# Moving the subtraction of the low parts, the first head's rotation, the partial sums of squares and the cut of the last output tiles

## The chip, the cores and the metric

The kernel runs on one core of a Trainium2 chip. TensorE (PE) multiplies matrices, VectorE (DVE), ScalarE (ACT) and GpSimd (POOL) work on elements, and SyncE (SP), POOL and ACT issue transfers (DMA). The metric is the device time of one execution in microseconds (us).

## The reference

The program is one inference step of a trunk of two layers (width 1024). It has 592 tokens: 16 meta tokens and 512 prompt tokens in one sequence, and 8 running sequences of 8 new tokens each. Each layer computes, in float32:

```
xn = rmsnorm(x, ln_g)
q, k, v, z_a, x_b, z_b, g_a, g_b = split(xn @ w_in)
q, k = rope(q), rope(k) * DK ** -0.5
ret  = chunked retention with decay, 4 heads, state S        # q k^T * decay @ v + q @ S
o_a  = group_norm(ret) * silu(z_a)
o_b  = rglru(causal_conv(x_b)) * silu(z_b)
x   += (sig(g_a) * (o_a @ w_a) + sig(g_b) * (o_b @ w_b)) @ w_o
```

At the end comes `y = rmsnorm(x, final_gain)`. The retention states, the convolution's last rows and the recurrent vectors are outputs too.

## The kernel before, in words

Every float32 factor is split into a high part (ACT rounds it by a copy) and a low part (the value less the high part). A product is then three matmuls into the same bank: high by high, weight's low by high, weight's high by low. The tokens lie along the free axis, so a tile of 128 output features is made of two halves of 296 tokens (288 in layer 1 where the meta tokens aren't needed), each of 8 steps of three matmuls, 24 in all.

The weights come in units of 128 x 1024. SP loads unit u when unit u-4 has been used; ACT makes `w_hi`, DVE `w_lo`, three units ahead of use. Four banks of PSUM serve as a ring: a half of a tile can start only when DVE has read what stood in its bank.

A layer begins with four heads (phase R). Head 0 is special. Its q and k tiles (units 0 to 3) are made from x times gain, not yet divided by the root of the mean square, so that PE can start before that root is there. The division is put into the cosines and sines (`trig`). Meanwhile the normalised xn is made for everything that follows: DVE multiplies (`norm(k)`, one of 8 tiles, into `xnf` with two buffers), ACT copies to `xn_hi`, and POOL subtracts to get `xn_lo` (lines 597 to 602); `norm(k)` waits for the subtraction of tile k-2. The root needs the sum over all 1024 features of the squares: ACT squares 8 tiles, DVE adds them into one or two partial sums (`GROUP`), and PE multiplies these by a matrix of ones (`square_sums`), placed at the step `sums_at` of `project_first`.

In head 0 DVE turns q by the angles right after q's second tile (lines 1168, 1169), fills `qz` and `qt` (lines 1179, 1185), and does the same for k after the fourth tile. PE transposes k through PSUM (`keys`), DVE scales it (`ktok`), ACT and DVE split it (`ktok_hi`, `ktok_lo`, lines 791, 792, 1229, 1230). Then DVE signals `ktok_ready`.

What follows for the 8 running sequences goes over SP's queue, in this order for each head: three transfers `k_scr<-ktok`, a weight unit, two transfers to `kst`, three of `v_scr<-vtok`, and, when those have landed, two of `vst<-v_scr`. Only when `vst` has landed may PE start `grow(0)` (line 1729), which stands between the tiles 8 and 9 of the head. PE's queue is in order, so everything behind waits with it.

The last phase (O) projects the merged branches by w_o. In layer 1 its last four tiles (features 512 to 1023) are run first for the first half of the tokens (`n` = 0), then for the second (`n` = 1), so that the first half's root and results are made while PE works on the second. DVE's queue in that stretch holds new x, the partial sum, the reciprocal and the results of the first half, in a fixed order. After the last matmul come, one behind another: new x, its square, the sum by ones, the square root, the reciprocal, four results and their transfers.

Of the kernel before, what the change touches and what calls it, by code (L numbers as in the profile page):

```python
# [36 lines left out]
T = TP + TS  # L37
# [29 lines left out]
WARM = 10  # L67
# [8 lines left out]

def cut_of_norm(n):
    return HALVES if n < DEPTH else cut(DEPTH - 1)
# [142 lines left out]
def trunk(nc, x_in, w_units, gate_w, packs, final_gain, consts, decay, state_ret,  # L221
# [7 lines left out]
    with ctx:  # L229
# [195 lines left out]
        GROUP = [4] + [KT] * DEPTH  # L425
        NORM_AT = {1: (0, 1), 2: (2, 3), 3: (4, 5), 4: (6,), 5: (7,)}

        def buffer(n, k):
            return k % 2
# [39 lines left out]
        def _(sp):  # L469
# [77 lines left out]
            for n, (a, b) in enumerate(cut(DEPTH - 1)):  # L547
                for k in range(0, KT, 2):
                    sp.wait_ge(y_ready, n * (KT // 2) + k // 2 + 1)
                    sp.dma_start(y_out.rearrange("p (k t) -> p k t", k=KT)[:, k:k + 2, a:b], yT[:, k:k + 2, a:b])\  # L550
                        .then_inc(y_stored, 16)
# [4 lines left out]
        def _(pool):  # L556
# [13 lines left out]
            for l in range(0, DEPTH):  # L570
# [7 lines left out]
                for h in range(0, HEADS):  # L578
# [17 lines left out]
                    if h == 0:  # L596
                        for k in range(KT):
                            pool.wait_ge(xnh_ready, l * KT + k + 1)
                            apart(pool)
                            pool.tensor_tensor(xn_lo[:, k, :], xnf[:, k % 2, :], xn_hi[:, k, :].bitcast(f32), SUB)\  # L600
                                .then_inc(xn_ready, 1)
                        pool.drain()
# [90 lines left out]
        def _(act):  # L693
# [57 lines left out]
            for l in range(0, DEPTH):  # L751
# [7 lines left out]
                for h in range(0, HEADS):  # L759
# [10 lines left out]
                    for i in range(11):  # L770
# [13 lines left out]
                        if i == 2:  # L784
                            act.wait_ge(qk_ready, hh * 2 + 1)
                            act.activation(qt_hi[:, :, :], qt[:, :, :], ACT.Copy)
                            act.activation(qk_hi[:, 0:2, :], qk[:, 0:2, :], ACT.Copy)
                            act.drain().then_inc(qkh_ready, 1)
# [213 lines left out]
            for n, (a, b) in enumerate(cut(DEPTH - 1)):  # L1002
# [11 lines left out]
        def _(dve):  # L1014
# [47 lines left out]
            for k in range(KT):  # L1062
                dve.drain()
                add_square(0, k)
            first_lo(2)

            for l in range(0, DEPTH):
# [24 lines left out]

                def norm(k):

                    if k >= 2:
                        dve.wait_ge(xn_ready, l * KT + k - 1)
# [4 lines left out]
                for h in range(0, HEADS):  # L1101
# [42 lines left out]
                    for i in range(11):  # L1144
                        turn = rot_k if h == 0 and i == 3 else rot
                        if i < 4:
# [19 lines left out]
                            if i % 2:  # L1166
                                a = first if i == 1 else 0
# [5 lines left out]
                            if i == 1:  # L1173
# [14 lines left out]
                            if i % 2:  # L1188
# [28 lines left out]
                        if h == 0:  # L1217
                            for k in {2: (2, 3), 3: (4, 5), 4: (6,), 5: (7,)}.get(i, ()):
                                norm(k)
                        if i == 4:  # L1220
# [337 lines left out]
                def new_x(it, i, n):  # L1558
                    a, b = cut(l)[n]
# [25 lines left out]
            def result(n, k):  # L1585
                a, b = cut(DEPTH - 1)[n]
# [9 lines left out]
            def last_square(n, k):  # L1596
                a, b = cut(DEPTH - 1)[n]
# [22 lines left out]
        def _(pe):  # L1620
# [15 lines left out]
            def project(ph, l, it, tile, i, which=(0, 1), left=None):  # L1636
# [4 lines left out]
                for n in which:  # L1641
                    a, b = (HALVES if every else cut(l))[n]
# [58 lines left out]
            for l in range(0, DEPTH):  # L1701
                for h in range(0, HEADS):
# [68 lines left out]
                    if h == 0:  # L1771
                        project_first("R", l, h, xg_ready, 0, raw, *((10, 5, True) if l == 0 else (5, 3)))
# [174 lines left out]
            for n in range(2):  # L1947
                for i in range(4):
                    if (n, i) == (1, 1):
                        square_sums(DEPTH, (0,))  # L1950
                    project("O", DEPTH - 1, 1, ("proj", i), i, (n,))
# [106 lines left out]
```

## Time and profile before

| what | value |
|---|---|
| median of 3 runs | 1938.37 us (1937.81 to 1938.79) |
| the profiled execution | 1938.32 us, its span 1936.5 us |
| PE busy | 1918.5 us, 99% of the span |
| DVE busy | 1181.5 us, 61% |
| ACT busy | 742.3 us, 38% |
| POOL busy | 265.2 us, 14% |
| chain that ended last | PE 86%, DVE 5%, ACT 4% |

The span is the time from the first to the last instruction in the trace. The profiled execution takes 1.8 us more than its span. Busy time of PE comprises the time in which a matmul's result drains, so two matmuls overlap in the rows; the distance between two starts is the price of one in a row of many. A number in brackets at the end of a row is the engine's idle time before that instruction and what ended it. A transfer's issue is shown at the queue that issues it (SPq), its landing in the chain.

### The profile page before, as it was taken

How to read it: one execution, taken by the hardware profiler on the slowest of the kernel's cores; microseconds unless marked ns; L12 is line 12 of the kernel's file. 1: busy time of each engine (PE TensorE's matmuls, PEld its weight loads, DVE VectorE, ACT ScalarE, POOL GpSimd, SP SyncE). 2: the span in 40 equal slices, each digit the busy share in tenths (PEclk: the TensorE clock that was granted, in tenths of full speed). 3: DMA queues.
4: the chain of work that ended last, by engine and by line, in shares of the span. 5: the costliest groups of instructions: out<-in, count | busy, mean ns of one | idle time of the engine just before them, and what ended most of it. 6: DMA issues, size and time to landing. Idle time of an engine off the chain costs nothing.

```text
span 1936.5 us, 32128 instructions
## 1 busy us (share of the span) xinstructions
PE 1918.5 (99%) x13184; PEld 1797.3 (93%) x13184; DVE 1181.5 (61%) x2008; ACT 742.3 (38%) x1149; POOL 265.2 (14%) x375
## 2 busy tenths in 40 slices
PE   8999999999999999999999999999999999999998
PEld 8889898898899999999998988988988999999997
DVE  8665665565666887424486655656556678853345
ACT  5332322323336766422343223233223367754223
POOL 2221120120231200000021201202102422000000
PEclk9999999999999999999999999999999999999999
DMA  6434533453343333322255335534534533342222
GB/s 216 134 115 163 178 125 125 162 169 112 130 155 99 105 105 107 123 77 77 88 170 168 126 126 169 168 112 134 178 116 137 167 98 104 101 135 79 84 81 81
DMA packets 105856, 247.01 MB, mean 128 GB/s; under 512 B 10830, under 2 KB 51134, under 8 KB 105326
## 3 DMA queue, kind: packets, MB, share of 16 engines
q1 hardware_dynamic: 78590, 149.74, 25.0%
q0 software_dynamic: 26976, 95.22, 14.9%
q8 instruction: 104, 1.70, 0.4%
q14 instruction: 42, 0.34, 0.1%
q10 hardware_dynamic: 144, 0.00, 0.0%
HBM read 186.10 MB, written 49.12 MB: 121 GB/s over the span
## 4 chain that ended last, share of the span: by engine, by line
PE 86%; DVE 5%; ACT 4%; DVEq 1%; DMA 1%; ACTq 1%; issue 1%; SPq 0%
PE bank L1624 21%; PE bank L1626 20%; PE bank L1625 20%; PE bank L1694 5%; PE bank L1696 5%; PE bank L1695 5%; PE last L1712 1%; PE last L1694 1%; PE last L1695 1%; PE last L1696 1%; PE bank L1852 1%; PE sums L1729 1%; DVE ct L1416 1%; DVE w_lo L462 1%; DVE rr L1469 1%
## 5 line engine op out<-in xcount | busy, mean ns | idle before, releaser
L1624 PE MATMUL bank<-xn_hi,w_hi 128*128 128x296 f32 (+1 forms) x2432 | 727.5, 299 | 0.2
L1626 PE MATMUL bank<-xn_lo,w_hi 128*128 128x296 f32 (+1 forms) x2432 | 722.4, 297 | 0.0
L1625 PE MATMUL bank<-xn_hi,w_lo 128*128 128x296 f32 (+1 forms) x2432 | 721.5, 297 | 0.0
L1624 PEld LDWEIGHTS bank<-xn_hi,w_hi 128*128 128x128 f32 x2432 | 457.3, 188 | 5.9 <-issue 4.3
L1625 PEld LDWEIGHTS bank<-xn_hi,w_lo 128*128 128x128 f32 x2432 | 457.8, 188 | 0.4
L1626 PEld LDWEIGHTS bank<-xn_lo,w_hi 128*128 128x128 f32 x2432 | 456.8, 188 | 0.0
L462 DVE TENSOR_TENSOR w_lo<-w_raw,w_hi 128x1024 fp32r<-128x1024 f32 x245 | 300.3, 1228 | 184.8 <-ACT w_hi L454 177.1
L454 ACT ACTIVATE w_hi<-w_raw 128x1024 fp32r<-128x1024 f32 x245 | 257.7, 1055 | 362.2 <-DMA w_raw<-in_w_units 357.7
L1624 PE MATMUL bank<-oa_hi,w_hi 128*128 128x296 f32 (+1 forms) x512 | 153.7, 300 | 0.0
L1625 PE MATMUL bank<-oa_hi,w_lo 128*128 128x296 f32 (+1 forms) x512 | 151.9, 297 | 0.0
L1626 PE MATMUL bank<-oa_lo,w_hi 128*128 128x296 f32 (+1 forms) x512 | 151.7, 296 | 0.0
L1624 PE MATMUL bank<-ob_hi,w_hi 128*128 128x296 f32 (+1 forms) x384 | 113.9, 297 | 0.0
L1625 PE MATMUL bank<-ob_hi,w_lo 128*128 128x296 f32 (+1 forms) x384 | 113.9, 297 | 0.0
L1626 PE MATMUL bank<-ob_lo,w_hi 128*128 128x296 f32 (+1 forms) x384 | 113.8, 296 | 0.0
L1694 PE MATMUL bank<-w_hi,xn_hi 128*128 128x512 f32 x256 | 100.9, 394 | 0.7 <-DVE rot_k L1160 0.7
L1696 PE MATMUL bank<-w_lo,xn_hi 128*128 128x512 f32 x256 | 100.8, 394 | 0.0
L1695 PE MATMUL bank<-w_hi,xn_lo 128*128 128x512 f32 x256 | 100.8, 394 | 0.0
L1624 PEld LDWEIGHTS bank<-oa_hi,w_hi 128*128 128x128 f32 x512 | 96.3, 188 | 3.9 <-issue 3.9
L1625 PEld LDWEIGHTS bank<-oa_hi,w_lo 128*128 128x128 f32 x512 | 96.3, 188 | 0.0
L1626 PEld LDWEIGHTS bank<-oa_lo,w_hi 128*128 128x128 f32 x512 | 96.3, 188 | 0.0
L592 POOL DMA_DIRECT2D out_ret_s<-S x64 | 45.9, 719 | 328.9 <-DVEq L1119 183.8
L767 ACT ACTIVATE zz<-bank 128x296 f32<-128x296 f32 (+1 forms) x64 | 26.5, 414 | 119.8 <-PE bank L1626 119.2
(286 smaller groups left out, 3083.7 us busy)
## 6 DMA issues: line engine op xcount, KB each, us to landing
w_raw<-in_w_units SPq DMA_DIRECT2D x215, 512.0 KB, 3.6
S<-in_state_ret POOLq DMA_DIRECT2D x64, 512.0 KB, 4.8
out_ret_s<-S POOLq DMA_DIRECT2D x64, 512.0 KB, 6.2
w_raw<-in_w_units SPq DMA_DIRECT2D x66, 256.0 KB, 3.2
vst<-v_scr SPq DMA_DIRECT2D x8, 512.0 KB, 4.1
out_ret_p<-Sp POOLq DMA_DIRECT2D x8, 512.0 KB, 5.9
v_scr<-vtok_hi SPq DMA_DIRECT2D x16, 160.0 KB
dec<-in_decay POOLq DMA_DIRECT2D x9, 264.0 KB, 5.1
```

What stands on the lines that cost most here:

```text
L454: act.activation(w_hi[:, n % RING, :], w_raw[:, n % RING, :], ACT.Copy).then_inc(unit_hi, 1)
L462: dve.tensor_tensor(w_lo[:, n % RING, :], w_raw[:, n % RING, :], w_hi[:, n % RING, :].bitcast(f32), SUB).then_inc(unit_lo, 1)
L592: pool.dma_start(dst, S[:, s, :, :]).then_inc(s_out[s], 16)
L767: act.activation(zz[:, i - 8, a:b], psum_of("R", name)[:, 0:b - a], ACT.Tanh, scale=0.5)\
L1416: dve.scalar_tensor_tensor(ct[:, 0:wide], xpad[:, t, j:j + wide], w(j), ct[:, 0:wide], MUL, ADD)
L1469: dve.tensor_tensor_scan(rr[:, t, :], aa[:, t, :], ii[:, t, :], 0.0, MUL, ADD)
L1624: pe.matmul(ps, w_hi[:, slot, cols], x_hi, start=first, stop=False)
L1625: pe.matmul(ps, w_lo[:, slot, cols], x_hi, start=False, stop=False)
L1626: return pe.matmul(ps, w_hi[:, slot, cols], x_lo, start=False, stop=last)
L1694: pe.matmul(ps, left_hi, right_hi, start=first, stop=False)
L1695: pe.matmul(ps, left_lo, right_hi, start=False, stop=False)
L1696: return pe.matmul(ps, left_hi, right_lo, start=False, stop=last)
```

## The change

Six edits, all in the same program:

1. `xn_lo` is subtracted by DVE (`norm_lo`) instead of POOL. `norm(k)` from k = 2 on begins with a drain of DVE in place of the wait for POOL.
2. In head 0 of each layer the rotation of q, with `qz` and `qt`, moves from unit 1 to unit 2 in DVE's order, between `norm(2)` and `norm(3)`; ACT's copies `qt_hi` and `qk_hi` move behind `xn_hi` of the tiles 4 and 5.
3. In front of layer 0 the squares are added into four partial sums of two tiles instead of two of four. Four additions remain of six, and drains between them go; PE's multiplications by ones become eight from four (a float32 matmul shows as two in the trace).
4. The sum by ones stands at step 9 instead of 10 in layer 0, and at step 6 instead of 5 in layer 1.
5. PE's warming matmuls before the first real one are 12 instead of 10.
6. The last four output tiles are cut into 336 and 240 tokens instead of 288 and 288.

```diff
-WARM = 10
+WARM = 12
+LAST = ((N_META, N_META + 336), (N_META + 336, T))
 def cut_of_norm(n):
-    return HALVES if n < DEPTH else cut(DEPTH - 1)
+    return HALVES if n < DEPTH else LAST
...
-        GROUP = [4] + [KT] * DEPTH
+        GROUP = [2] + [KT] * DEPTH
...
         def buffer(n, k):
-            return k % 2
+            return k // 2 % 2 if GROUP[n] == 2 else k % 2
...
-                    if h == 0:
-                        for k in range(KT):
-                            pool.wait_ge(xnh_ready, l * KT + k + 1)
-                            apart(pool)
-                            pool.tensor_tensor(xn_lo[:, k, :], xnf[:, k % 2, :], xn_hi[:, k, :].bitcast(f32), SUB)\
-                                .then_inc(xn_ready, 1)
-                        pool.drain()
...
-                        if i == 2:
+                        if i == (2 if h else 3):
                             act.wait_ge(qk_ready, hh * 2 + 1)
                             act.activation(qt_hi[:, :, :], qt[:, :, :], ACT.Copy)
...
             for k in range(KT):
-                dve.drain()
                 add_square(0, k)
...
+                def norm_lo(k):
+
+                    dve.wait_ge(xnh_ready, l * KT + k + 1)
+                    dve.tensor_tensor(xn_lo[:, k, :], xnf[:, k % 2, :], xn_hi[:, k, :].bitcast(f32), SUB)\
+                       .then_inc(xn_ready, 1)
+
                 def norm(k):
 
                     if k >= 2:
-                        dve.wait_ge(xn_ready, l * KT + k - 1)
+                        dve.drain()
...
                         if h == 0:
-                            for k in {2: (2, 3), 3: (4, 5), 4: (6,), 5: (7,)}.get(i, ()):
+                            if i == 1:
+                                norm_lo(0)
+                                norm_lo(1)
+                            if i == 2:
+                                norm(2)
+                                rotated(0, rot, first)
+                                norm(3)
+                                queries_apart()
+                                dve.drain().then_inc(qk_ready, 1)
+                                norm_lo(2)
+                                norm_lo(3)
+                            for k in {3: (4, 5), 4: (6,), 5: (7,)}.get(i, ()):
                                 norm(k)
+                            for k in {3: (4, 5), 4: (6,), 5: (7,)}.get(i, ()):
+                                norm_lo(k)
...
-                        project_first("R", l, h, xg_ready, 0, raw, *((10, 5, True) if l == 0 else (5, 3)))
+                        project_first("R", l, h, xg_ready, 0, raw, *((9, 5, True) if l == 0 else (6, 3)))
...
-                    project("O", DEPTH - 1, 1, ("proj", i), i, (n,))
+                    project("O", DEPTH - 1, 1, ("proj", i), i, (n,), None, LAST)
```

`rotated` and `queries_apart` hold the instructions of lines 1168 to 1171 and 1174 to 1187, unchanged. The other uses of `cut(DEPTH - 1)` in the last stretch become `LAST` as well.

DVE in head 0 of layer 0, before, from the first two tiles of `xnf` to the first product with q's fellow k. `rot` is q's second tile times sine and cosine, `L462` makes `w_lo`.

```order
L1097 SCALAR_TENSOR_TENSOR xnf<-acc,lp,rstd 128x592 x2
L1168 TENSOR_TENSOR qk<-qk,rot 128x592
L1169 TENSOR_TENSOR qk<-qk,rot 128x592
L1179 TENSOR_TENSOR qz<-qk,cst 128x4x8 x4
L1185 TENSOR_TENSOR qt<-qk,cst 128x32
L462 TENSOR_TENSOR w_lo<-w_raw,w_hi 128x1024
L1155 TENSOR_TENSOR qk<-bank,trig 128x296
```

The same place after; `L465` makes `w_lo`, `L1091` is the new `xn_lo`, and `L1156` and `L1157` read the third projected tile.

```order
L1098 SCALAR_TENSOR_TENSOR xnf<-acc,lp,rstd 128x592 x2
L465 TENSOR_TENSOR w_lo<-w_raw,w_hi 128x1024
L1091 TENSOR_TENSOR xn_lo<-xnf,xn_hi 128x592 x2
L1156 TENSOR_TENSOR qk<-bank,trig 128x296
L1157 TENSOR_TENSOR qk<-bank,trig 128x296
L1156 TENSOR_TENSOR qk<-bank,trig 128x296
L1157 TENSOR_TENSOR qk<-bank,trig 128x296
L465 TENSOR_TENSOR w_lo<-w_raw,w_hi 128x1024
L1098 SCALAR_TENSOR_TENSOR xnf<-acc,lp,rstd 128x592
L1169 TENSOR_TENSOR qk<-qk,rot 128x592
L1170 TENSOR_TENSOR qk<-qk,rot 128x592
L1098 SCALAR_TENSOR_TENSOR xnf<-acc,lp,rstd 128x592
```

The weight's low part and the reading of the third tile now stand ahead of q's rotation, and each pair of `xnf` is followed by its pair of `xn_lo`.

ACT in the same head, before, from the second pair of `xn_hi` to the `w_hi` that DVE needs next (`L786` and `L787` are q's copies, `L773` is k's).

```order
L757 ACTIVATE xn_hi<-xnf 128x592 x2
L786 ACTIVATE qt_hi<-qt 128x32
L787 ACTIVATE qk_hi<-qk 128x1184
L454 ACTIVATE w_hi<-w_raw 128x1024
L757 ACTIVATE xn_hi<-xnf 128x592 x2
L773 ACTIVATE qk_hi<-qk 128x1184
L454 ACTIVATE w_hi<-w_raw 128x1024
```

And after (`L457` makes `w_hi`, `L753` `xn_hi`, `L783` is q's copy, `L769` k's):

```order
L457 ACTIVATE w_hi<-w_raw 128x1024
L753 ACTIVATE xn_hi<-xnf 128x592 x2
L782 ACTIVATE qt_hi<-qt 128x32
L783 ACTIVATE qk_hi<-qk 128x1184
L769 ACTIVATE qk_hi<-qk 128x1184
L457 ACTIVATE w_hi<-w_raw 128x1024
```

Both copies of 1184 columns now stand between the third pair of `xn_hi` and the next `w_hi`.

## Rows read from the trace of the kernel before

**Rows 1.** The page, part 1: busy time, share of the span, instructions.
```profile
PE 1918.5 (99%) x13184; PEld 1797.3 (93%) x13184; DVE 1181.5 (61%) x2008; ACT 742.3 (38%) x1149; POOL 265.2 (14%) x375
```

**Rows 2.** Waits of PE, whole span: us in total, times, longest.
```profile
PE bank L1624 <- DVE qk L1156: 1.8, 2, 1.7
PE sums L1685 <- DVE sqs L1035: 1.6, 2, 1.0
...
PE sums L1729 <- DMA vst<-v_scr: 1.0, 1, 1.0
PE sums L1743 <- DVEq L1189: 0.7, 1, 0.7
```

**Rows 3.** PE in order of time, head 0 of layer 0: start, us, what.
```profile
6.37 0.61 PE L1624 MATMUL bank<-xg_hi,w_hi 128*128 128x296 f32 x1 [0.65 <-DVE w_lo L1054]
...
80.98 0.49 PE L1729 MATMUL sums<-vst,kst 24*128 24x512 f32 x2 [0.95 <-DMA vst<-v_scr]
```

**Rows 4.** SP's queue in order of time, the same head.
```profile
65.81 0.77 SPq L502 DMA_DIRECT2D k_scr<-ktok_hi  x1
```

**Rows 5.** The chain that ended last, layer 0 and layer 1.
```profile
76.60 4.33 DMA vst<-v_scr
...
1037.24 4.14 DMA vst<-v_scr
...
1041.42 0.49 PE sums L1729
```

**Rows 6.** DVE in order of time, layer 0.
```profile
18.34 2.51 DVE L1035 TENSOR_TENSOR sqs<-sqs,sq 128x592 f32<-128x592 f32 x3 [0.77 <-ACT sq L710]
...
22.75 2.00 DVE L1019 RECIPROCAL rstd<-rstd 128x296 f32<-128x296 f32 x1 [0.43 <-ACT rstd L701]
...
35.45 2.05 DVE L1169 TENSOR_TENSOR qk<-qk,rot 128x592 f32<-128x592 f32 x1
37.64 1.53 DVE L1179 TENSOR_TENSOR qz<-qk,cst 128x32 f32<-128x32 f32 x4
...
46.51 2.10 DVE L1168 TENSOR_TENSOR qk<-qk,rot_k 128x592 f32<-128x592 f32 x1
...
59.08 1.88 DVE L462 TENSOR_TENSOR w_lo<-w_raw,w_hi 128x1024 fp32r<-128x1024 f32 x1
```

**Rows 7.** The same operations of DVE in head 1 of layer 0.
```profile
166.52 0.78 DVE L1168 TENSOR_TENSOR qk<-qk,rot 128x592 f32<-128x592 f32 x1
167.22 0.77 DVE L1169 TENSOR_TENSOR qk<-qk,rot 128x592 f32<-128x592 f32 x1
168.13 0.50 DVE L1179 TENSOR_TENSOR qz<-qk,cst 128x32 f32<-128x32 f32 x4
```

**Rows 8.** POOL in order of time, layer 0.
```profile
34.93 3.89 POOL L600 TENSOR_TENSOR xn_lo<-xnf,xn_hi 128x592 fp32r<-128x592 f32 x2 [8.57 <-ACT xn_hi L757]
```

**Rows 9.** PE, DVE in order of time, head 0 of layer 1.
```profile
982.73 1.26 PE L1685 MATMUL sums<-sqs,ones 128*128 128x296 f32 x4 [0.55 <-DVE sqs L1035]
...
989.60 0.46 DVE L1155 TENSOR_TENSOR qk<-bank,trig 128x288 f32<-128x288 f32 x1
...
1015.79 1.36 DVE L462 TENSOR_TENSOR w_lo<-w_raw,w_hi 128x1024 fp32r<-128x1024 f32 x1 [1.23 <-ACT w_hi L454]
...
1026.10 0.41 DVE L1230 TENSOR_TENSOR ktok_lo<-ktok,ktok_hi 80x256 fp32r<-80x256 f32 x1
```

**Rows 10.** DVE in order of time, the end of the program.
```profile
1921.33 1.42 DVE L1588 TENSOR_TENSOR yT<-yT,rstd 128x576 f32<-128x576 f32 x2
...
1926.22 0.46 DVE L1562 SCALAR_TENSOR_TENSOR acc<-bank,xT 128x288 f32<-128x288 f32 x1 [0.38 <-PE bank L1626]
1928.58 1.95 DVE L1019 RECIPROCAL rstd<-rstd 128x288 f32<-128x288 f32 x1 [1.90 <-ACT rstd L701]
1930.61 2.77 DVE L1588 TENSOR_TENSOR yT<-yT,rstd 128x576 f32<-128x576 f32 x4
```

**Rows 11.** A stretch at the end: us, each engine's busy time, granted clock, DMA.
```profile
1932.00:1933.00 1.00, 0.00 (x0) 0.00 (x0) 1.00 (x3) 0.00 (x0) 0.00 (x0) 0.55 0.72 253
```

More of the change, by code:

```diff
@@ L546, in _ @@
                         value_stack(hh)
-            for n, (a, b) in enumerate(cut(DEPTH - 1)):
+            for n, (a, b) in enumerate(LAST):
                 for k in range(0, KT, 2):
@@ L1001, in _ @@
                         split_hi(act, "O", l, it, i)
-            for n, (a, b) in enumerate(cut(DEPTH - 1)):
+            for n, (a, b) in enumerate(LAST):
                 for k in range(4, KT):
@@ L1165, in _, with rotated @@
                             dve.drain()
-                            if i % 2:
-                                a = first if i == 1 else 0
+                            def rotated(at, turn, a):
                                 dve.tensor_tensor(qk[:, at, a:], qk[:, at, a:], turn[:, 0, a:], SUB)
@@ L1172, in _, with queries_apart @@
                                 dve.drain()
-                            if i == 1:
+                            def queries_apart():
                                 dve.wait_ge(const_in, 32)
@@ L1187, in _ @@
                                                   .rearrange("p (o t) -> p o t", o=1).to_broadcast([P, 2, TAILP]), MUL)
-                            if i % 2:
+                            if i == 3:
+                                rotated(2, turn, 0)
+                            if i == 1 and h:
+                                rotated(0, turn, first)
+                                queries_apart()
+                            if i == 3 or i == 1 and h:
                                 dve.drain().then_inc(qk_ready, 1)
@@ L1217, in _ @@
                         if h == 0:
-                            for k in {2: (2, 3), 3: (4, 5), 4: (6,), 5: (7,)}.get(i, ()):
+                            if i == 1:
[5 more added lines that the diff above has]
+                                norm(3)
+                                queries_apart()
+                                dve.drain().then_inc(qk_ready, 1)
+                                norm_lo(2)
+                                norm_lo(3)
+                            for k in {3: (4, 5), 4: (6,), 5: (7,)}.get(i, ()):
                                 norm(k)
+                            for k in {3: (4, 5), 4: (6,), 5: (7,)}.get(i, ()):
+                                norm_lo(k)
                         if i == 4:
@@ L1558, in new_x @@
                 def new_x(it, i, n):
-                    a, b = cut(l)[n]
+                    a, b = (LAST if (l, it) == (DEPTH - 1, 1) else cut(l))[n]
                     k, name = it * 4 + i, (("proj", i), n)
@@ L1585, in result @@
             def result(n, k):
-                a, b = cut(DEPTH - 1)[n]
+                a, b = LAST[n]
                 dve.wait_ge(yg_ready, 4 * (n + 2) if k >= 4 else 4)
@@ L1596, in last_square @@
             def last_square(n, k):
-                a, b = cut(DEPTH - 1)[n]
+                a, b = LAST[n]
                 add_square(DEPTH, k, slice(a, b), DEPTH * KT + 4 + n * 4 + (k - 3))
@@ L1634, in wait_unit, with project @@
                 pe.wait_ge(unit_lo, l * UNITS_LAYER + it * p.units + (p.unit0 + i + 1))
-            def project(ph, l, it, tile, i, which=(0, 1), left=None):
+            def project(ph, l, it, tile, i, which=(0, 1), left=None, columns=None):
                 x_hi, x_lo = left or (xn_hi, xn_lo)
@@ L1641, in project @@
                 for n in which:
-                    a, b = (HALVES if every else cut(l))[n]
+                    a, b = (columns or (HALVES if every else cut(l)))[n]
                     name = (tile, n)
```

## The prediction

> **What bounds the kernel now.** I read the page first: PE is busy for 99% of the span [rows 1], so no engine can give much, and what can be won or lost lies in PE's few waits. I then read PE's waits over the whole span [rows 2]. Four kinds stand out: for a bank that DVE frees (1.8 us), for the partial sums of squares (1.6), for `vst` (1.0), for the rotated k (0.7). The order of time places them: all of the first kind, the last two and 1.0 us of the second are in head 0 of layer 0; layer 1 has one gap of 0.55 us [rows 9]. The third view is the chain around `vst`. In layer 0, PE waits 0.95 us at 80.98 for its landing [rows 3], and in layer 1 the chain goes through the same transfer at 1041.42, where PE arrives just then [rows 5]. Going back from there, SP's queue starts the series of transfers the moment DVE has finished `ktok_lo`: at 65.81 in layer 0 [rows 4]; in layer 1 that row ends at 1026.10 + 0.41 = 1026.5 [rows 9]. From `ktok_ready` to the start of line 1729 pass 15.2 and 14.9 us. These are issues and landings of transfers, and the change touches none. So the time at which `ktok_ready` comes, not the time at which PE is through, sets when PE passes line 1729 in both layers. It is the end of DVE's queue in head 0. I hold the change against that.
>
> The profiled execution takes 1938.3 us, 1.8 more than its span, and the median shown is 1938.4, so no correction is needed.
>
> **DVE's queue in head 0.** Start to start, DVE needs 0.69 us for a `tensor_tensor` of 592 columns (166.52 to 167.22) [rows 7].
>
> - Added: eight `xn_lo`, 8 x 0.69 = 5.5 us per layer.
> - Added: six drains ahead of `norm(2)` to `norm(7)`. Without one, the next instruction starts 0.08 us before the row of the last ends (167.22 against 167.30); with one, 0.14 behind (167.99 to 168.13, two drains' worth of signalling in it, other places nearer 0.1) [rows 7]. I take 0.18 each, 1.1 us.
> - Given back: DVE instructions that ran while POOL subtracted were long. POOL was at it from 34.93 to 38.82 [rows 8], and the rotation in it took 2.05 us against 0.77 in head 1, the four `qz` 1.53 against 0.50, the other rotation 2.10 against 0.78, a `w_lo` 1.88 against 1.23 as elsewhere [rows 6, 7]. That is 1.28 + 1.03 + 1.32 + 0.65 = 4.3; two smaller ones (another `w_lo`, `ktok_lo`) I put at 0.6 together: 4.9 us per layer. POOL no longer has elementwise work there, so all of it goes.
> - Added: DVE now waits for ACT between `xnf` and its low part where the two are alone in the queue. ACT's copy takes 0.7, so for tiles 6 and 7 each time about 0.75; for tile 5 about 0.2. And the two copies of 1184 columns stand between `xn_hi` of tile 5 and `w_hi` of unit 7, so DVE waits some 1.1 us for that `w_hi`. Together 2.9, where the queue before waited 1.23 [rows 9] and 0.75 later for ACT, 2.0. In layer 1 a unit's landing adds 0.3. So +0.9 and +1.2.
>
> That is 5.5 + 1.1 - 4.9 + 0.9 = +2.6 in layer 0 and +2.9 in layer 1.
>
> **Where the queue starts.** In layer 0 the squares come sooner. Before, ACT waited for DVE's additions, and the last ended at 18.34 + 2.51 = 20.85 [rows 6]. With two partial sums more and no drains, ACT can square the eight tiles in a row from 13.8 (0.59 each, to 18.5), and the last addition ends at 19.4. PE reaches step 9 at 18.4; sixteen passes of 0.25 us take it to 22.4, but those for the first half of the tokens are through at 20.4, result at 20.6. ACT's table load now ends at 20.8 and the root at 21.5, so the reciprocal starts at 21.5 instead of 22.75: -1.3. PE pays 2.0 us more for the ones matmuls and saves the wait of 1.0, and the wait of 1.7 for the bank shrinks to about 0.1, so it too is ahead by 1.3.
>
> In layer 1 the sum moves behind another step. PE would have waited 0.55 [rows 9]; instead it runs 12 matmuls, 1.6 us. PE is 0.55 ahead, but the sum and with it the root come 1.6 - 0.55 = 1.05 later: DVE reads the first bank at 990.6 instead of 989.60. PE then waits for that bank for 1.0.
>
> So `ktok_ready` moves by -1.3 + 2.6 = **+1.3 us in layer 0** (67.1) and by +1.05 + 2.9 = **+3.9 us in layer 1** (1030.4). PE gets nearer in layer 0: the k rotation ends at 47.3, keys start at 47.8 rather than 49.5, and it stands before line 1729 at 78.8 and waits till 82.3. What hid the later `ktok` before was that PE itself came only at 80.0; that cover is what the gain ahead turns into, a wait of 3.5 us. In layer 1 it comes at 1041.8 and waits till 1045.3. Behind that wait stand tile 9, the scores and everything else. The bounds: with drains at 0, no added waits for ACT and all contention back (5.5), layer 0 gives -1.3 and layer 1 +1.0; with half of the contention only and waits of 1 us more each, +4.8 and +7.4.
>
> The Trainium skill, "VectorE: DVE Perf Modes", section "The DRAIN you can't avoid", says that an operation never starts before the pipeline of the last is empty, signalled or not. By it the six explicit drains would cost nothing, layer 0 would come at +0.2 and layer 1 at +2.8, the whole 2.2 us earlier than my sum. The starts in rows 7 overlap where no drain stands, so here it does not hold.
>
> **The first microseconds.** Two more warming matmuls of 0.43 us fill the 0.65 that PE idles before 6.37 [rows 3]; the first real one starts when `w_lo` is there, as before. Between -0.5 (a sooner rise of the clock) and +0.3, I take 0.
>
> **The end.** Behind the last matmul all pieces shrink by 48 of 288 columns: new x 0.05, square 0.04, sum 0.08, root 0.04, the reciprocal of 1.95 by 0.31, four results of 2.77 by 0.39 [rows 10]: 0.9 us. But the first half grows as much, and its sum stands at PE behind (0,7) and (1,4). (n,k) is half n, tile k: (1,4) ends at 1917.2 instead of 1915.65, since four tiles of 336 lie ahead of it. From there DVE's queue is a chain: root of 336 columns and square of (1,4) at 1919.2, reciprocal 2.25 to 1921.8, new x (1,5) 1921.9, its square by ACT, two results of 0.83 to 1924.7, new x (1,6), square, two results to 1927.5. Before, DVE idled 0.38 us ahead of the last new x at 1926.22 [rows 10]; now PE has the tile at 1926.4 and DVE takes it at 1927.5, +1.25. With -0.9 behind it DVE ends 0.35 later; the last transfers are a sixth smaller, -0.25. **+0.1 us**, between -1.0 (the queue hides after all) and +0.9. That a matmul of 240 columns keeps the price per column is in these bounds.
>
> **Sum.** 1938.3 + 1.3 + 3.9 + 0 + 0.1 = 1943.6 us.
>
> **Rivals.**
>
> A: `ktok_ready` isn't what `vst` hangs on, and the transfers follow PE. For it: the values' stacks stand in the same series, and these come from PE. Against: SP's first row starts with `ktok_ready` to the hundredth [rows 4], and the rest follows without PE. Then layer 0 gives what PE is ahead at the keys, -1.7, less 0.5 for a wait for the last `xn_lo`, layer 1 +0.5 (the 1.0 for the bank less the 0.55), the end +0.1: 1937.7 us, not slower. It decides if `ktok_ready` moves by less than PE's arrival does.
>
> B: the long rows of DVE are not POOL's doing and stay long. Then the 4.9 us are not given back in either layer: 1943.6 + 9.8 = 1953.4. Against it: 2.05 beside 0.77 for the same shape, with POOL's row right above it.
>
> C: the waits of 3.5 us cost the clock as well. After PE's last matmul at 1928.0 the granted clock falls to 0.55, the lower of its two levels, in the microsecond from 1932 on [rows 11]; PE had then run nothing for 4 us, and 3.5 is close to that. Each such wait would then be followed by some us at 1.2 GHz, at 1.5 us lost each: 1946.6.
>
> D: ACT and DVE interleave better than I lay out and the drains are cheap, so that layer 0 is even and layer 1 costs 2: 1940.4, within 0.2%.
>
> **How the numbers follow.** A difference of 0.2% is 3.9 us, about what a measurement tells from none; slower starts at 1942.2. My forecast has 0.52, C 0.10, B 0.03, A 0.12, D 0.23. The forecast's own range is 1941.5 to 1945.5, a tenth of it under 1942.2. A lies within 0.2% save for a quarter, in which the end gains too. Slower: 0.47 + 0.10 + 0.03 + a tenth of D, 0.62. Faster: a quarter of A, 0.03. Same: 0.35. The range, from D's middle to C, is 1939.2 to 1946.8.
>
> **What will show it.** In the trace after: POOL has no `xn_lo`; the rotations take 0.77; `k_scr` starts at 67.1 and the reciprocal at 21.5 in layer 0; PE's waits list 3 to 4 us twice for `vst`, and the gaps before the keys are gone; in layer 1 PE waits 1.0 for the first bank and `ktok_lo` ends at 1030.4 + the shift of layer 0; the last new x starts 1 us behind PE. If PE's waits for `vst` are under 1.5 us, the step from `ktok_ready` to `vst` is wrong, and the time will be under 1940.

## The result and the profile after

| | median | lowest to highest | runs |
|---|---|---|---|
| after | 1947.56 us | 1946.77 to 1947.91 | 5 |
| before, same chip | 1938.79 us | 1937.81 to 1939.75 | 5 |

The ratio is 1.0043, with a 95% interval from 1.0032 to 1.0054: the change makes the kernel 0.43% slower. The profiled execution takes 1947.56 us, its span 1945.7, 9.2 more than before. I had predicted 1943.6 with a range of 1939.2 to 1946.8. The direction was right, the size was not.

The page, part 1, against [rows 1]:

```profile
PE 1922.7 (99%) x13196; PEld 1801.0 (93%) x13196; DVE 1183.0 (61%) x2022; ACT 742.3 (38%) x1149; POOL 239.2 (12%) x359
```

The waits of PE over the whole span (us in total, times, longest), against [rows 2]:

```profile
PE sums L1750 <- DMA vst<-v_scr: 6.3, 2, 3.3
PE bank L1645 <- DVE xg_lo L1036: 2.0, 3, 1.0
PE bank L1715 <- DVE rot_k L1161: 1.7, 1, 1.7
PE sums L1710 <- ACT sq L1002: 1.6, 1, 1.6
PE sums L1721 <- DVEq L1018: 1.1, 1, 1.1
PE bank L1645 <- DVE qk L1157: 1.0, 1, 1.0
```

The wait for `vst`, 1.0 us once, has become 6.3 us in two waits. Two more follow from what was forecast: the wait for the first bank of layer 1 (`qk`, 1.0), and the longer one for ACT's square behind the last new x (1.6, before 0.6), since DVE takes that x later. The gap of 0.7 ahead of the keys is gone as forecast, but the one for `rot_k`, just before it, has grown from 0.7 to 1.7: PE's lead in layer 0 is spent there, ahead of the wait for `vst`. The three waits for `xg_lo` lie in the first 13 us and cost nothing; the part on the prediction tells why.

DVE in order of time, head 0 of layer 0, against [rows 6] (start, us, operation, and in brackets the idle time before it):

```profile
22.36 2.00 DVE L1015 RECIPROCAL rstd<-rstd 128x296 f32<-128x296 f32 x1 [0.42 <-ACT rstd L697]
...
38.56 1.23 DVE L465 TENSOR_TENSOR w_lo<-w_raw,w_hi 128x1024 fp32r<-128x1024 f32 x1
39.88 0.83 DVE L1098 SCALAR_TENSOR_TENSOR xnf<-acc,lp,rstd 128x592 f32<-128x592 f32 x1
40.63 0.77 DVE L1169 TENSOR_TENSOR qk<-qk,rot 128x592 f32<-128x592 f32 x1
41.31 0.77 DVE L1170 TENSOR_TENSOR qk<-qk,rot 128x592 f32<-128x592 f32 x1
...
42.95 0.49 DVE L1181 TENSOR_TENSOR qz<-qk,cst 128x32 f32<-128x32 f32 x4
...
43.67 1.46 DVE L1091 TENSOR_TENSOR xn_lo<-xnf,xn_hi 128x592 fp32r<-128x592 f32 x2
...
55.71 1.23 DVE L465 TENSOR_TENSOR w_lo<-w_raw,w_hi 128x1024 fp32r<-128x1024 f32 x1 [1.10 <-ACT w_hi L457]
...
58.63 0.78 DVE L1091 TENSOR_TENSOR xn_lo<-xnf,xn_hi 128x592 fp32r<-128x592 f32 x1 [0.77 <-ACT xn_hi L753]
```

Both rotations and `qz` have the short duration that head 1 showed before. The pair of `xn_lo` takes 1.46 us. The waits for ACT are there with 1.10 and 0.77.

SP's queue in order of time, the first transfer of the series in layer 0 (against [rows 4]) and in layer 1:

```profile
68.07 0.77 SPq L505 DMA_DIRECT2D k_scr<-ktok_hi  x1
...
1033.76 0.78 SPq L505 DMA_DIRECT2D k_scr<-ktok_hi  x1
```

PE in order of time, head 0 of layer 0, from the wait on, against [rows 3], and the same line in layer 1:

```profile
82.96 0.50 PE L1750 MATMUL sums<-vst,kst 24*128 24x512 f32 x2 [3.01 <-DMA vst<-v_scr]
...
84.18 0.30 PE L1647 MATMUL bank<-xn_lo,w_hi 128*128 128x296 f32 x1
84.32 0.35 PE L1645 MATMUL bank<-xn_hi,w_hi 128*128 128x296 f32 x1
...
85.20 0.45 PE L1646 MATMUL bank<-xn_hi,w_lo 128*128 128x296 f32 x1
85.45 0.45 PE L1647 MATMUL bank<-xn_lo,w_hi 128*128 128x296 f32 x1
...
1048.80 0.50 PE L1750 MATMUL sums<-vst,kst 24*128 24x512 f32 x2 [3.29 <-DMA vst<-v_scr]
```

The first matmuls behind the wait follow each other at 0.14 us, but from 84.5 on at 0.25. The stretches of the same time say why (us and the length; busy time of PE, weight load, DVE, ACT, POOL, with instructions in brackets; then the granted clock, DMA share, GB/s):

```profile
83.00:84.00 1.00, 1.00 (x8) 0.76 (x9) 0.49 (x1) 0.00 (x0) 0.00 (x0) 1.00 1.05 422
84.00:85.00 1.00, 1.00 (x8) 1.00 (x7) 1.00 (x3) 0.81 (x1) 0.00 (x0) 0.71 0.51 201
85.00:86.00 1.00, 1.00 (x6) 1.00 (x6) 1.00 (x2) 0.25 (x1) 0.00 (x0) 0.50 0.00 0
86.00:88.00 2.00, 2.00 (x10) 2.00 (x10) 1.36 (x2) 0.00 (x0) 0.00 (x0) 0.54 0.00 0
88.00:90.00 2.00, 2.00 (x16) 1.58 (x15) 1.06 (x3) 0.42 (x1) 0.00 (x0) 1.00 0.04 8
```

Each line gives a stretch from start to end. The granted clock falls to 0.50, that is 1.2 instead of 2.4 GHz, for some 3.4 us, beginning 1.5 us after PE has resumed. In layer 1 the same stands behind the wait:

```profile
1050.00:1051.00 1.00, 1.00 (x8) 1.00 (x7) 1.00 (x3) 0.00 (x0) 0.00 (x0) 0.70 0.62 246
1051.00:1053.00 2.00, 2.00 (x10) 2.00 (x9) 1.98 (x3) 1.06 (x1) 0.00 (x0) 0.50 0.03 12
1053.00:1054.00 1.00, 1.00 (x6) 0.98 (x5) 0.32 (x1) 0.00 (x0) 0.00 (x0) 0.59 0.08 16
```

DVE at the end of the program, against [rows 10]:

```profile
1936.46 0.40 DVE L1583 SCALAR_TENSOR_TENSOR acc<-bank,xT 128x240 f32<-128x240 f32 x1
1938.60 1.65 DVE L1015 RECIPROCAL rstd<-rstd 128x240 f32<-128x240 f32 x1 [1.74 <-ACT rstd L697]
1940.34 2.37 DVE L1609 TENSOR_TENSOR yT<-yT,rstd 128x480 f32<-128x480 f32 x4
```

The last new x has no idle time before it any more: DVE's own chain sets it. What lies behind it is shorter, as the prediction laid out.

**Where the 9.2 us are.** Differences of the two profiles: PE passes `vst` in layer 0 at 82.96 against 80.98, +1.98. The clock behind it loses 1.46 (3.44 later stands what DVE does in layer 1 just ahead of the sum). PE passes `vst` in layer 1 at 1048.80 against 1041.42, +7.38, of which 3.94 are layer 1's own. The clock behind it loses 1.58 (the new x of the last phase stands +8.96). The end adds 0.37, the last transfers take 0.15 off.

### The profile page after: what moved, and what is told of

It reads as the page before. It is cut to its first block, busy times and chain, and to the rows that moved or that the text cites. A ratio compares the mean times of both kernels' runs of the same rounds, so it can differ in the third digit from the quotient of the medians.

```text
span 1945.7 us, 32136 instructions
## 1 busy us (share of the span) xinstructions
PE 1922.7 (99%) x13196; PEld 1801.0 (93%) x13196; DVE 1183.0 (61%) x2022; ACT 742.3 (38%) x1149; POOL 239.2 (12%) x359
## 4 chain that ended last, share of the span: by engine, by line
PE 83%; DVE 7%; ACT 4%; DVEq 2%; DMA 2%; ACTq 1%; issue 1%; SPq 1%
PE bank L1645 21%; PE bank L1647 20%; PE bank L1646 20%; PE bank L1715 5%; PE bank L1717 5%; PE bank L1716 5%; PE last L1733 1%; PE last L1715 1%; PE last L1717 1%; PE last L1716 1%; DVE w_lo L465 1%; PE bank L1873 1%; PE sums L1750 1%; DVE ct L1437 1%; DVE xnf L1098 1%
## 5 line engine op out<-in xcount | busy, mean ns | idle before, releaser
L1645 PE MATMUL bank<-xn_hi,w_hi 128*128 128x296 f32 (+3 forms) x2432 | 728.9, 300 | 0.2
L1647 PE MATMUL bank<-xn_lo,w_hi 128*128 128x296 f32 (+3 forms) x2432 | 724.0, 298 | 0.0
L1646 PE MATMUL bank<-xn_hi,w_lo 128*128 128x296 f32 (+3 forms) x2432 | 722.9, 297 | 0.0
L465 DVE TENSOR_TENSOR w_lo<-w_raw,w_hi 128x1024 fp32r<-128x1024 f32 x245 | 298.8, 1222 | 188.1 <-ACT w_hi L457 179.8
L457 ACT ACTIVATE w_hi<-w_raw 128x1024 fp32r<-128x1024 f32 x245 | 257.8, 1055 | 367.7 <-DMA w_raw<-in_w_units 363.3
L1645 PEld LDWEIGHTS bank<-ob_hi,w_hi 128*128 128x128 f32 x384 | 72.3, 188 | 0.0
```

The lines of the kernel that those rows point to most:

```text
L457: act.activation(w_hi[:, n % RING, :], w_raw[:, n % RING, :], ACT.Copy).then_inc(unit_hi, 1)
L465: dve.tensor_tensor(w_lo[:, n % RING, :], w_raw[:, n % RING, :], w_hi[:, n % RING, :].bitcast(f32), SUB).then_inc(unit_lo, 1)
L1645: pe.matmul(ps, w_hi[:, slot, cols], x_hi, start=first, stop=False)
L1646: pe.matmul(ps, w_lo[:, slot, cols], x_hi, start=False, stop=False)
L1647: return pe.matmul(ps, w_hi[:, slot, cols], x_lo, start=False, stop=last)
```

## The experiments

I held one theory: `ktok_ready`, the end of DVE's queue in head 0, is late; PE waits for `vst` some 3 us, and the wait costs the clock as well. Its rivals: the clock has nothing to do with the wait; or one of the other parts (the later rotation, the sums, the cut) costs the time by itself. Each ratio is to the kernel before, run beside it on the same chip; brackets hold the 95% interval.

### The low parts back on POOL

`x1_low_on_pool`: the kernel after with part 1 undone.

```diff
+                            pool.tensor_tensor(xn_lo[:, k, :], xnf[:, k % 2, :], xn_hi[:, k, :].bitcast(f32), SUB)\
+                                .then_inc(xn_ready, 1)
...
-                                norm_lo(k)
```

> The changed kernel, with one part undone: xn_lo is subtracted by POOL again, and norm(k) waits for it; the later rotation of q and all else stay. Theory (DVE's queue in head 0 sets when ktok_ready comes, that sets when vst lands, and a wait of 3 us for it costs the clock as well): the queue loses eight subtractions (5.5 us) and six drains, and gets back some 4 to 5 us of long rows per layer, so ktok_ready comes 1.5 to 2.5 us sooner in each layer than in the changed kernel, PE's waits for vst fall to about 1 us, the granted clock stays whole, and the time is 1939 to 1942 us. Rival (the side edits, above all the sum by ones at a later step in layer 1 and the new cut, cost the time): it stays within 2 us of 1947.6.

Measured: 1938.9 us, 1.0004 [0.9995, 1.0013]. `k_scr` starts at 64.73 and 1026.08, and PE passes `vst` at 79.84 and 1041.03 after waits of 1.66 and 0.15 us, with the granted clock at 1.00 behind. The two rows of layer 0:

```profile
64.73 0.77 SPq L505 DMA_DIRECT2D k_scr<-ktok_hi  x1
...
79.84 0.50 PE L1750 MATMUL sums<-vst,kst 24*128 24x512 f32 x2 [1.66 <-DMA vst<-v_scr]
```

So the loss needs part 1, and the other five together bring nothing without it. From the reciprocal to `k_scr` pass 42.7 us in layer 0 here, 45.7 in the kernel after (in layer 1 42.1 and 45.5): the subtraction on DVE costs 3.0 and 3.4 us of its queue. That is less than its eight rows take, since with POOL at work again DVE has long rows again, now at other operations. While POOL subtracts from 34.19 to 37.99 and from 40.73 to 42.51, a `w_lo` takes 2.24 us and an `xnf` 1.88, where the kernel after has 1.23 and 0.83 for the same two:

```profile
36.84 2.24 DVE L465 TENSOR_TENSOR w_lo<-w_raw,w_hi 128x1024 fp32r<-128x1024 f32 x1
...
41.27 1.88 DVE L1105 SCALAR_TENSOR_TENSOR xnf<-acc,lp,rstd 128x592 f32<-128x592 f32 x1
```

### The low parts and the rotation alone

`x2_low_and_rotation_only`: the kernel before with parts 1 and 2.

```diff
-                            pool.tensor_tensor(xn_lo[:, k, :], xnf[:, k % 2, :], xn_hi[:, k, :].bitcast(f32), SUB)\
-                                .then_inc(xn_ready, 1)
...
+                                rotated(0, rot, first)
+                                norm(3)
+                                queries_apart()
```

> The kernel before with only the low parts on DVE and the first head's rotation later. Theory: ktok_ready comes 2.6 us later in layer 0 and 3.0 us in layer 1, PE waits 3 to 4 us for vst in each layer, the clock falls to half behind both waits at 1.5 us each: 1938.8 + 2.6 + 3.0 + 3.0 = 1947.4 us. Rival (the four other edits carry the loss): within 2 us of 1938.8.

Measured: 1949.31 us, 1.0057 [1.0042, 1.0072], 1.9 above the expectation. PE waits 2.94 and 2.71 us for `vst`, and behind both the clock falls to 0.50. By the medians the parts 3 to 6 are worth about 1.8 us beside the parts 1 and 2, though the intervals of the two ratios overlap. No kernel has part 1 without the later rotation, so how the loss divides between these two isn't shown.

### Busy instead of waiting

`x3_busy_wait`: the kernel after, in head 0 of each layer with twelve matmuls of ones by ones, which nothing reads, ahead of the wait for `vst`. PE's wait for a free buffer (`kt_free`) moves ahead of them too.

```diff
+                        for _ in range(12):
+                            pe.matmul(sums[0][:, 0:P], ones[:, :], ones[:, :], start=True, stop=True)
                     pe.wait_ge(st_in, hh * 64 + 64)
```

> The changed kernel, with 12 matmuls of ones by ones (128x128, into a bank that is free) put between PE's tile 8 with the products behind it and its wait for vst in head 0 of each layer, 2.6 us in waits of 3.0 and 3.3. They compute nothing that is used. Theory: vst lands when it did, so the wait ends at the same time, but the clock does not fall: -1.5 us in each layer, 1944.6 us, and the granted clock is whole behind both. Rival (the fall of the clock follows from something else, or the matmuls delay PE): no gain, or slower by up to 2 us.

Measured: 1944.89 us, 1.0034 [1.0022, 1.0047], 2.7 us less than the kernel after. PE in order of time and the stretches behind:

```profile
78.99 2.94 PE L1816 MATMUL sums<-ones 128*128 128x128 f32 x24
82.42 0.50 PE L1750 MATMUL sums<-vst,kst 24*128 24x512 f32 x2 [0.48 <-DMA vst<-v_scr]
```

```profile
84.00:86.00 2.00, 2.00 (x17) 2.00 (x16) 2.00 (x4) 0.56 (x1) 0.00 (x0) 1.00 0.08 27
86.00:88.00 2.00, 2.00 (x16) 1.59 (x16) 1.95 (x4) 0.42 (x1) 0.00 (x0) 1.00 0.00 0
```

PE gets on no sooner than `vst` lets it, and does 24 useless passes more in each layer, yet the program is faster: the clock stays at 1.00 behind both waits. That is the cost of the idle time, apart from the wait itself.

### The cut of the last tiles alone

`x4_cut_only`: the kernel before with part 6.

```diff
+LAST = ((N_META, N_META + 336), (N_META + 336, T))
```

> The kernel before with only the last four output tiles in parts of 336 and 240 columns. Theory: DVE's queue binds the last stretch, its last new x starts 1.2 us later, the pieces behind are 0.9 shorter, the transfers 0.1 to 0.2 shorter: +0.1 to +0.3 us, 1939.0. Rival (the cut shortens everything behind the last matmul): -0.9 us, 1937.9, and the last new x starts within 0.3 us of PE's last matmul.

Measured: 1938.32 us, 1.0000 [0.9991, 1.0009]. DVE's chain reaches the last new x at 1927.68, before at 1926.22, without idle time before it, and loses there what the shorter pieces behind give. The step of the prediction (+0.1) holds as far as the runs can tell.

### ACT's order

`x5_act_weight_first`: the kernel after with `w_hi` of unit 7 ahead of the two copies of 1184 columns in head 0.

```diff
+                        if i == 4 and h == 0:
+                            split_hi(act, "R", l, h, i)
...
-                        if i != 7:
+                        if i != 7 and (i != 4 or h):
```

> The kernel after, but ACT makes w_hi of unit 7 ahead of q's and k's two copies of 1184 columns in head 0 of each layer, so that DVE's wait of 1.1 us for it goes. If the end of DVE's queue sets when vst lands, ktok_lo ends about 1.1 us sooner in each layer and PE's waits for vst shrink from 3.0 and 3.3 us to about 1.9 and 2.2. Theory I (a wait of 3 us costs the clock, one of 2 does not): no fall of the granted clock behind either, 1947.6 - 2.2 - 3.0 = 1942.4 us. Theory II (the fall has nothing to do with the length): the clock falls still, 1945.4. Rival (vst follows PE or another part of the series): waits stay as they are, 1947.6.

Measured: 1944.5 us (1942.92 to 1947.55), 1.0031 [1.0021, 1.004]. DVE's wait of 1.1 us is gone and `ktok_lo` ends 1.1 us sooner against the reciprocal in both layers. PE waits 2.63 and 2.37 us, where I had expected 1.9 and 2.2. The clock falls behind the first and not behind the second:

```profile
82.00:83.00 1.00, 1.00 (x8) 1.00 (x7) 1.00 (x2) 0.66 (x1) 0.00 (x0) 0.75 0.91 365
83.00:85.00 2.00, 2.00 (x10) 2.00 (x10) 2.00 (x4) 0.40 (x1) 0.00 (x0) 0.50 0.00 0
```

```profile
1047.00:1049.00 2.00, 2.00 (x18) 2.00 (x17) 2.00 (x5) 1.06 (x1) 0.00 (x0) 1.00 0.27 104
```

My expectation of a clean limit between 2 and 3 us missed: it had no fall at all. The runs spread over 4.6 us, where before, beside it, spreads over 1.7. The profiled execution, 1942.92, is the fastest of the ten.

### Layer 1's sum back at step 5

`x6_sum_at_step_5`: the kernel after with layer 1's part of edit 4 undone (the end of one line, as in the cuts further down).

```diff
-*((9, 5, True) if l == 0 else (6, 3))
+*((9, 5, True) if l == 0 else (5, 3))
```

> The kernel after, with the sum of squares in layer 1 back at step 5. By my theory PE waits 0.55 us for the last partial sum again and the wait of 1.0 for the first bank goes, the root comes 0.8 us sooner, ktok_lo ends 0.8 us sooner and PE passes vst 0.8 us sooner, with a wait of about 2.9, behind which the clock falls still (2.7 was enough in the kernel with parts 1 and 2 alone): 1946.8 us. Rival (what counts is PE's own idle time ahead of the sum): 0.5 us slower than after, 1948.1.

Measured: 1947.81 us (1945.35 to 1950.18, 4 runs), 1.0044 [1.003, 1.0058]. Its four runs form two pairs, 1945.4 and 1945.7, 1949.9 and 1950.2, so this decides nothing by its time. What parts the pairs isn't shown; the profile is of the faster one and has one fall of the clock, behind layer 1's wait of 2.90. It is of use, though: from the start of the reciprocal to `k_scr` pass 47.1 us in layer 1, in the kernel after 45.5. Where the 1.6 come from is told with the next two kernels. Layer 0, the same code as after, has a wait of 2.35 here, since `vst` landed 0.6 us sooner behind `k_scr`, and no fall of the clock.

### Without the low parts, the sum and the cut, and then with ACT's order

`x7_rotation_and_layer0_sums`: `x1_low_on_pool` with layer 1's sum back at step 5 and the last tiles back at 288; `x8_rotation_sums_act` the same with ACT's order of `x5_act_weight_first`.

> The kernel before with the later rotation and the earlier sum of layer 0 (parts 2, 3, 5 and part 4 for layer 0): the low parts stay on POOL, the sum of layer 1 stays at step 5, the last tiles at 288. From 1938.9 us with the low parts on POOL, less 0.8 for layer 1 and 0.35 for the end: 1937.8. If the rotation's later place costs something of its own in layer 1, 1938.7, as before.

> The kernel of the run with the rotation and layer 0's sums, with ACT's w_hi of unit 7 ahead of the two copies. ktok_lo ends some 1.1 us sooner; the wait of 1.7 us for vst in layer 0 shrinks to 0.6, and in layer 1, where PE waits hardly, little is won: 1936.5 us. If w_hi was not what DVE waited for with the low parts on POOL, 1937.8.

Measured: 1940.49 us (1939.75 to 1944.22), 1.0012 [1.0003, 1.0021], and 1938.14, 0.9996 [0.9987, 1.0005]. Both are above what I expected, and their profiles show two reasons. The first is the clock, in the first kernel alone: there PE waits 1.64 us at 80.39 and the clock falls; the kernel with the low parts on POOL had waited 1.66 at 79.84 without a fall. This profile is of an execution of 1942.9, one of four from 1942.9 to 1944.2; the other seven lie at 1939.8 to 1941.5, and whether the clock fell in those no profile shows:

```profile
81.00:82.00 1.00, 1.00 (x7) 1.00 (x8) 1.00 (x2) 0.00 (x0) 0.00 (x0) 0.77 0.98 397
82.00:84.00 2.00, 2.00 (x10) 2.00 (x9) 2.00 (x4) 1.06 (x1) 0.00 (x0) 0.50 0.07 29
```

The second reason, in both, is a weight. DVE in layer 1, first in that kernel, then in the one with the low parts on POOL (step 6):

```profile
985.25 3.87 DVE L1022 RECIPROCAL rstd<-rstd 128x296 f32<-128x296 f32 x2 [0.38 <-ACT rstd L704]
...
1002.95 1.23 DVE L465 TENSOR_TENSOR w_lo<-w_raw,w_hi 128x1024 fp32r<-128x1024 f32 x1 [3.24 <-ACT w_hi L457]
```

```profile
983.97 3.87 DVE L1022 RECIPROCAL rstd<-rstd 128x296 f32<-128x296 f32 x2 [1.13 <-ACT rstd L704]
...
998.21 2.23 DVE L465 TENSOR_TENSOR w_lo<-w_raw,w_hi 128x1024 fp32r<-128x1024 f32 x1
```

The later rotation has put a `w_lo` ahead of it in DVE's queue, and that one hangs on a weight unit that lands late: ACT can begin its `w_hi` only 16.6 us behind the reciprocal, where it is 12.0 in the other kernel. Every profile with the sum at step 6 has 12.0 us (six of them), while with step 5 seven of eight, the one of before among them, have 16.4 to 17.1. Before, the rotation stood ahead of that `w_lo` and covered the wait. In that kernel and in before one of the unit transfers takes 9.1 and 8.9 us to land, in the two with step 6 and the low parts on POOL (`x1_low_on_pool` and `x10_rotation_sums_step6`, below) 4.4 and 5.1 at most; POOL's four state loads of 512 KB stand in the same stretch in all of them.

### The rotation in layer 0 only, and step 6

`x9_rotation_layer0_only` has parts 2, 3, 5, step 9 and ACT's order in layer 0 and leaves layer 1 as before. `x10_rotation_sums_step6` has them in both layers, with layer 1's sum at step 6. One line of the first against the kernel after, and the one line in which the second differs from `x8_rotation_sums_act`:

```diff
-                            if i == 1 and h:
+                            if i == 1 and (h or l):
```

```diff
-*((9, 5, True) if l == 0 else (5, 3))
+*((9, 5, True) if l == 0 else (6, 3))
```

> The kernel before with the later rotation, the four partial sums, step 9 and ACT's w_hi of unit 7 ahead of the two copies, all of it in layer 0 alone; layer 1 as before. In the run with the same in both layers PE passes vst in layer 0 at 78.2, 2.8 us sooner than before, and then loses 1.8 of it in layer 1, where DVE waits 3.1 us for a w_hi that the rotation had covered. If that is the loss, layer 1 costs nothing here: 1939.1 - 2.8 = 1936.3 us. Rival (PE gives the 2.8 back at another wait in layer 1): 1938.1, as the run with both layers.

> The kernel of the run with rotation, sums and ACT's order in both layers, with layer 1's sum at step 6 as in the kernel after. If step 6 lets the weight of unit 5 land before ACT needs it, DVE's wait of 3.1 us at the second w_lo of layer 1 is gone, as in the kernel with the low parts on POOL (none there), ktok_lo ends some 1.2 us sooner against the start of the reciprocal, and PE stands before vst hardly at all: 1939.1 - 2.8 + 0.8 = 1937.1 us. If step 6 only delays the root (my prediction's view), it is 0.8 later than the run with step 5: 1938.9.

Measured: 1937.23 us, 0.9991 [0.9982, 1.0000], and 1937.01 us, 0.9990 [0.9981, 0.9999]. In both, PE stands before `vst` in layer 1 without a wait, and in layer 0 with one of 0.25 and 0.79. In the second, DVE reads that weight without idle time, as step 6 had let me expect, and the time is the expected one; my prediction's view of step 6 as a mere delay doesn't hold in this kernel. The first lies between its two expectations: PE passes `vst` at 78.86 in layer 0, since x landed late in this profile, 2.1 us sooner than before, and gives 0.3 of it back in layer 1. Both are 1.6 and 1.8 us below before, at the edge of what the runs can tell. They have the lowest medians of all kernels here.

### The spread

`x11_rotation_busy_wait` is `x7_rotation_and_layer0_sums` with six matmuls by ones ahead of the wait, `x12_act_and_busy_wait` is `x5_act_weight_first` with eight.

```diff
+                        for _ in range(6):
+                            pe.matmul(sums[0][:, 0:P], ones[:, :], ones[:, :], start=True, stop=True)
```

> The run with rotation and layer 0's sums (low parts on POOL), whose times lay between 1939.8 and 1944.2 and whose profile shows waits of 1.64 and 2.19 us for vst and a fall of the clock behind the first: six matmuls by ones ahead of the wait in head 0 of each layer, which nothing reads. If its spread is the clock behind these waits, the times are close together and at its lower end, 1940.3, with the clock at 1.00 behind both waits. If the spread has another cause, it stays.

> The kernel after with ACT's w_hi of unit 7 ahead of the two copies and eight matmuls by ones ahead of the wait for vst in head 0 of each layer, which nothing reads. The waits of 2.6 and 2.4 us are then 1.0 and 0.7, and the clock stays: 1947.6 - 2.5 (sooner ktok_ready) - 3.0 (clock) = 1942.1 us, with little spread where the run without them had 1942.9 to 1947.6. If the clock was not the cause of that spread, 1944.5.

Measured: 1939.24 us (1938.78 to 1941.02, where it was 1939.75 to 1944.22) and 1941.84 us (1940.6 to 1942.79, where it was 1942.92 to 1947.55); ratios 1.0004 [0.9994, 1.0013] and 1.0015 [1.0006, 1.0024]. In both profiles the clock is 1.00 behind both places. The medians fall by 1.3 and 2.7 us although PE is given more to do; of this 0.3 is the kernel before, which was that much faster beside them. Both now spread over 2.2 us instead of 4.5 and 4.6. The clock behind the waits thus made much of the spread too, as far as one profile of each tells: before spread over 3.5 us in its 33 runs beside these two, and over 1.7 in the 27 earlier ones. The first comes out 1.1 us below its expectation. In its profile the weight landed early (the one of eight), which can be part of that.

## Why the prediction was wrong in size

**What held.** DVE's queue: from the reciprocal of layer 0 to the start of `k_scr` pass 43.06 us before and 45.71 after, +2.65 (predicted +2.6). In layer 1 42.5 and 45.5, +3.0 (predicted +2.9). Its terms are in the rows: `xn_lo` at 0.69 start to start, the rotations at 0.77, and what POOL had held up was given back. A drain costs what I took: `xnf` at 39.88 stands 0.09 behind the row before it, where the rotation at 40.63 starts 0.08 before its predecessor's row ends. The Trainium skill, "VectorE: DVE Perf Modes", section "The DRAIN you can't avoid", which my prediction set against this, says itself that a next operation that is not held starts earlier; I had read it too strictly. The Trainium skill, "SBUF — State Buffer", section "Who interferes with whom", says that a tensor_tensor of VectorE with both inputs in SBUF contends with GpSimd's reads for a shared pair of ports. By this rule the long rows had to go with POOL's work, and the trace agrees: 2.05 has become 0.77 in rows of one shape.

The sum by ones in layer 1: the root comes 4.20 later, 3.44 of it carried from layer 0, so 0.76 (predicted 1.05). The way from `ktok_ready` to `vst`: 14.9 and 15.1 us after `ktok_lo` (predicted 15.2 and 14.9). The end: DVE +0.37 (predicted 0.35). Rivals A and B are refuted: the transfers moved with `ktok_ready`, and the long rows went with POOL's subtractions and came back with them in `x1_low_on_pool`. D fails as well, since layer 0's queue grew by 2.65 us and isn't even.

The first microseconds gave nothing, as I took it, but they did change. From 6.67 on the matmuls stand 0.14 us apart, where before they stand 0.25 apart up to 10.3:

```profile
6.67 0.30 PE L1646 MATMUL bank<-xg_hi,w_lo 128*128 128x296 f32 x1
6.81 0.29 PE L1647 MATMUL bank<-xg_lo,w_hi 128*128 128x296 f32 x1
```

(The clock column shows 1.00 for both, so here the spacing tells.) PE then waits 2.0 us for `xg_lo` instead, and stands no nearer: its matmuls with the last pair of tiles begin 1.0 us behind that pair's `xg_hi` in both kernels (13.40 to 12.38 before, 14.30 to 13.29 after). The two more warming matmuls aren't shown to be the cause: `x2_low_and_rotation_only`, with 10 of them, has 0.14 from 6.4 on too.

**Smaller misses.** In layer 0 the start moved by -0.4, not -1.3. But x itself landed 0.9 us later in the profile after: from `xg_hi` of the last pair of tiles (12.38 and 13.29) to the reciprocal pass 10.37 us before and 9.07 after, a gain of 1.3 as worked out. Over the profiles of this study that `xg_hi` starts at 12.3 to 13.5, so this much of any single profile is chance. The way to `vst` was 0.3 shorter than I took, the last transfers 0.1 longer: 0.8 us over the forecast in all, apart from the clock. That layer 1 came out at 3.94 of 3.9 is partly luck: the root came 0.3 sooner than forecast, the queue took 0.1 and the way to `vst` 0.2 longer.

**The step that failed** is the price of the two waits. The prediction had them: 3.5 us each, now measured as 3.0 and 3.3. It then counted them as idle time alone and put what they do to the clock into rival C, "at 1.5 us lost each: 1946.6", with a chance of 0.10. Its sum has nothing for the clock. The runs showed 1.46 and 1.58 us in that place, and that C isn't a rival of the forecast but its consequence: all six waits for `vst` of 2.6 us and more, in four profiles, had the fall. The busy wait alone takes 2.7 us off. C's own 1.5 each was right, though no row of the kernel before showed how long such a fall lasts. Forecast plus 3.0 is 1946.6; the rest up to 1947.6 are the smaller misses, rounded.

Why I gave it a tenth: [rows 11] show the low level after 4 us without work, and I read that as a limit that 3.5 stays under. One row at 4 says that 4 is enough, not that less isn't. It was the nearest row, and it spoke for C. The ends of the other profiles show how little that 4 meant: the clock falls there too, 1.0 us behind PE's last matmul in `x4_cut_only` (which itself had waited 1.6 us for ACT), 1.7 in `x6_sum_at_step_5`, 3.2 in the kernel after and 4.4 in `x10_rotation_sums_step6`.

The range was too narrow for its own terms as well. I called it "from D's middle to C", but D stands at 1940.4, not 1939.2; and the upper bounds given for the two layers and the end add up to 1951.4.

**What stays open.** The length of the wait doesn't decide alone. In single profiles the clock fell behind waits for `vst` of 1.64, 2.63, 2.71, 2.90, 2.94, 3.01 and 3.29 us, and not behind 1.66, 2.19, 2.35 and 2.37; nor did it behind the wait of 1.7 for `rot_k`, which six profiles have. All of 2.6 and more fell; below, both occur, at the same length. Once, in `x4_cut_only`, it fell at 8.6 us behind waits of only 0.9 and 0.7, where PE had time to spare and nothing was lost. What else it hangs on (where the wait falls in time, or what PE did ahead of it) no run here isolates. That the state loads on POOL's queue make the weight unit late in layer 1 is read from rows and wasn't tested either: no kernel moved them.

## What to carry to other kernels

Where a forecast has PE wait some 3 us, price the wait twice, once for itself and once for the clock behind it; the two are one case, not two. Where the waits are of 1.6 to 2.4 us, give the fall a chance of its own and widen the range. Where such a wait can't be avoided, a few matmuls ahead of it that nothing reads can pay, as here. And what moved work adds to the queue of the engine whose last instruction releases a long series of transfers is paid there in full, even if that engine is 61% busy.

## What the runs showed of the hardware

- In the kernel after, the granted clock fell only 1.5 us after PE had resumed (resumed 82.96, spacing of matmuls 0.25 instead of 0.14 from 84.5 on) and stayed low for 3.4 us: the price appears behind the wait, in work that looks innocent. Over the seven falls behind a wait for `vst`, the start lies from 0.0 (`x6_sum_at_step_5`, layer 1) to 1.6 us behind PE's resuming, and the low stretch is 3.4 us long in every one.
- Two kernels with the same code up to there waited 1.64 and 1.66 us at the same place; one lost the clock and the other didn't. The three kernels whose waits lie in or reach into 1.6 to 2.6 us (`x5_act_weight_first`, `x6_sum_at_step_5`, `x7_rotation_and_layer0_sums`) spread over 4.6, 4.8 and 4.5 us, the kernel before beside them over 1.7.
- Matmuls of 240 columns followed each other at 0.111 us, those of 296 at 0.137: the price per column is the same.
- The longest landing of a transfer of weights of 256 KB at the start of layer 1 was 9.1 us in `x7_rotation_and_layer0_sums` and 5.1 in `x10_rotation_sums_step6`, whose transfers were issued 1.6 us sooner against the reciprocal (the first 2.3 instead of 3.9 us behind it). The sooner issue isn't all of it: in `x11_rotation_busy_wait`, issued at 3.9 us as well, the longest took 5.9.
